# A front written out as one order, with two engines computing the modulation vectors in turn

## The chip, the core and the metric

The kernel runs on one NeuronCore of a Trainium2 chip. TensorE (PE) multiplies, VectorE (DVE), ScalarE (ACT) and GpSimd (POOL) work beside it, and SyncE (SP) and GpSimd issue DMAs. Each engine takes its own instructions in order, and engines meet only at semaphores. Times are device microseconds (us) of one launch; the metric is the median over runs. Everything is float32, and a float32 matmul of the program stands in the trace as two matmul records. A change of less than about 0.2% of the time can't be told from none here.

## The reference

One sample of 512 latent tokens and 256 context tokens, width 1024, two layers. Every layer makes six modulation vectors (shift, scale, gate, twice) from the condition vector:

```python
sh1, sc1, g1, sh2, sc2, g2 = jnp.split((silu_c @ ada_w[l] + ada_b[l])[:, None, :], 6, axis=-1)
h = modulate(x, sh1, sc1)                      # rms_norm(x) * (1 + scale) + shift
if l % 2 == 0:
    y, y_c = even_mixer(h, modulate(ctx, csh1, csc1), ...)   # differential attention, spatial gating
else:
    y = conformer_conv(h, *conv_p)
x = x + g1 * y
x = x + g2 * peer_ffn(modulate(x, sh2, sc2), ...)
```

`even_mixer` projects to q, k, v, u and vg. For each of 4 heads it takes two softmaxes over 768 keys and multiplies `p0 - lam * p1` by v; the result is normalized per head, set beside the gated `u * mixed(vg)`, and projected by `w_out`. `peer_ffn` scores each token against 2 x 128 keys for 8 heads, takes the best 16 experts of 16384 per head, and for each token reads 128 rows of two tables (`w_down` and `w_up`, 8 KB for the pair), takes a dot product, a gelu, and a weighted sum.

## The kernel before

A class `Plan` makes a list of stages, each cut into phases, and `run_phases` walks this list on every engine, so that the list sets the order of work on all of them. Phases that stand beside a gather are issued on ACT and DVE two gathers later than on PE (`later`, `LOOK = 2`).

**The main loop.** For each layer and each block of 128 tokens there are 128 gathers. A gather is one indirect DMA on POOL's queue (128 rows of 8 KB) into one of 8 slots of `ring`, a dot product on DVE, three small activations on ACT (gelu, weight, a diagonal matrix `diag`), and 4 matmuls in 64x64 tiles on PE, which sum into `ffn_out`. `beside` puts the phases of the next block (norm, q projection, gating, attention, output projection, norm, selection of experts) between the gathers, spaced by the phases' costs. `attend` has 10 phases: in the phase of head h, DVE finds the peaks of head h+1's scores, waits for ScalarE's exponentials and combines the two softmaxes, while PE waits for head h's result, turns it and later multiplies it by v.

**The front.** Until the first gather of block 0, `ring` holds other things: `ht_all` (the modulated, turned inputs of all 6 token tiles), the context, and buffers for the modulation weights. It does, in this order: `ada` (shift and scale of layer 0, four 2 MB weight chunks through PE in 64x64 tiles), `front_norms`, `lam`, keys and values of 6 tiles in turn, q, gating, attention and projection of block 0, norm, selection. Beside it runs `side_ada`, the ten other modulation vectors: 20 chunks of 2 MB, each loaded by POOL's queue into one of two buffers and summed over its 8 slices of 128 input channels by DVE alone; PE only sums over partitions afterwards (four 128x2 products, or a 128x512 one for gate rows):

```python
for k in range(KD):
    weight, scale = buffers[c.buf][:, k, :], cond_silu[:, 0, k:k + 1]
    ...
        ins = dve.scalar_tensor_tensor(out=acc_j, in0=weight, scalar=scale, in1=acc_j,
                                       op0=ALU.mult, op1=ALU.add)
    step(ins)
```

The phases of `side_ada` are spread over the others by `spread`. All other weights (2 MB chunks) go through SP's queue into `weights`, which has 2 buffers; a chunk is loaded once the one before it in its buffer has been used. POOL's first gather waits for all of `side_ada` and for the first half of the selection. PSUM has three two-bank tiles used in rotation, and a fourth for the side work.

In the prediction "u0" to "u19" are the phases of the side work in the changed kernel, k0 to k12, v, q, a, g, p, n, s those of the keys, values, query, attention, gating, projection, norm and selection.

## Time and profile before

| | before |
|---|---|
| median of 3 runs | 3370.67 us (3367.43 to 3374.5) |
| profiled execution | 3375.42 us, of which the span 3373.6 us |
| first product of the keys | 72.7 us |
| first gather issued | 361.8 us |
| PE, DVE, ACT, POOL busy | 70%, 67%, 37%, 34% |
| moved by DMA | 1288.62 MB, mean 382 GB/s |
| mean granted TensorE clock | 0.787 of 2.4 GHz |

The busy shares are means over two parts that have little in common: the front, where few gathers can run, and the main loop after it. The stages must be read apart.

### The profile page before, as it was taken

Reading aid. Unit: us, or ns where it says so; the run is one execution under the profiler, and the core shown is the slowest. Engines: PE = TensorE matmul, PEld = TensorE weight load, DVE = VectorE, ACT = ScalarE, POOL = GpSimd, SP = SyncE. Lnnn points to the kernel's source line nnn. Section 1 sums busy time; section 2 is a strip of 40 time slices with the busy share of each in tenths; the row PEclk is TensorE's granted clock in tenths of the full one; section 3 lists DMA queues with packets and bytes.
Section 4 is the critical chain, followed back from the end, with each engine's and each line's share of the span. In section 5 each row is a group of like instructions: output and inputs, shape, how many; then the busy total and the mean of one; then the engine's idle time right before and its main releaser. Section 6 shows DMA issues by size and latency. Waiting matters only on the chain.

```text
span 3373.6 us, 37863 instructions
## 1 busy us (share of the span) xinstructions
PE 2348.5 (70%) x12920; PEld 992.8 (29%) x12920; DVE 2271.6 (67%) x5467; ACT 1250.3 (37%) x3679; POOL 1132.1 (34%) x1052
## 2 busy tenths in 40 slices
PE   5966577857776778596586695675577567766676
PEld 2435223512342234262133161251124112421111
DVE  2765855685648665847947749669956896595444
ACT  2111245334533463443343442333343333343333
POOL 0000233343333333333433433333433343344332
PEclk7977688878887789797787696786788677876666
DMA  6565899999999999999999999899999999999998
GB/s 256 217 257 195 341 391 370 421 404 418 377 422 419 398 372 414 385 379 402 421 382 421 413 388 394 336 402 384 421 389 418 421 420 377 422 420 418 421 421 354
DMA packets 167025, 1288.62 MB, mean 382 GB/s; under 512 B 19248, under 2 KB 20144, under 8 KB 23728
## 3 DMA queue, kind: packets, MB, share of 16 engines
q0 software_dynamic: 150912, 1124.14, 81.9%
q1 hardware_dynamic: 15920, 162.07, 11.5%
q8 instruction: 101, 1.65, 0.2%
q14 instruction: 92, 0.75, 0.1%
HBM read 1284.04 MB, written 2.10 MB: 381 GB/s over the span
## 4 chain that ended last, share of the span: by engine, by line
DVE 30%; DMA 27%; PE 27%; issue 8%; ACT 7%; POOL 1%; DVEq 0%; ACTq 0%; SPq 0%; POOLq 0%
DMA ring<-in_experts,expert 24%; DVE ring L1340 11%; PE psum L1645 10%; DVE arena L1226 7%; PE psum L1395 6%; PE psum L1409 3%; PE psum L1591 3%; PE psum L1376 1%; DMA x<-in_x 1%; ACT arena L804 1%; DVE arena L1252 1%; POOL ring L692 1%; ACT arena L855 1%; PE psum L1561 1%; ACT shares_of L942 1%
## 5 line engine op out<-in xcount | busy, mean ns | idle before, releaser
L1645 PE MATMUL psum<-ring,diag 64*64 64x512 f32 x8192 | 1395.1, 797 | 790.5 <-ACT diag L943 781.9
L692 POOL DMA_INDIRECT ring<-in_experts,expert x1024 | 1119.0, 1093 | 1927.2 <-PE psum L1645 1757.3
L1340 DVE CUSTOM_DVE_ANT_0 ring<-ring,h 128x1024 f32<-128x1024 f32 x1024 | 1220.3, 1222 | 640.5 <-DMA ring<-in_experts,expert 623.3
L1645 PEld LDWEIGHTS psum<-ring,diag 64*64 64x64 f32 x8192 | 301.0, 163 | 1733.2 <-ACT diag L943 1484.4
L941 ACT ACTIVATE acts<-dots 128x1 f32<-128x1 f32 x1024 | 206.2, 201 | 1577.7 <-DVE dots L1340 1525.6
L943 ACT ACTIVATE diag<-ident_half,shares_of 128x64 f32<-128x64 f32 x1024 | 356.0, 348 | 33.3
L942 ACT ACTIVATE shares_of<-acts,gate 128x1 f32<-128x1 f32 x1024 | 301.7, 295 | 33.2
L1409 PE MATMUL psum<-arena,weights 128*128 128x128 f32 x2048 | 270.4, 296 | 30.1 <-DMA weights<-in_chunks 30.1
L1409 PEld LDWEIGHTS psum<-arena,weights 128*128 128x128 f32 x2048 | 259.1, 209 | 83.3 <-issue 47.8
L1226 DVE SCALAR_TENSOR_TENSOR arena<-kept,taps,arena 128x128 f32<-128x128 f32 x960 | 263.2, 343 | 2.3
L1395 PE MATMUL psum<-weights,arena 128*128 128x512 f32 x400 | 188.7, 616 | 3.6 <-ACTq L807 2.5
L718 ACT ACTIVATE arena<-psum 128x128 f32<-128x128 f32 (+2 forms) x86 | 64.6, 751 | 214.5 <-PE psum L1409 88.9
L1376 PE MATMUL psum<-ident,arena 128*128 128x128 f32 x464 | 90.2, 355 | 59.7 <-DVE arena L1082 36.0
L1591 PE MATMUL psum<-arena,weights 128*128 128x256 f32 x512 | 119.4, 386 | 0.6 <-ACTq L807 0.6
L1395 PE MATMUL psum<-weights,ring 128*128 128x512 f32 x240 | 110.6, 615 | 2.4 <-DMA weights<-in_chunks 1.8
L677 POOL DMA_DIRECT2D ring<-in_chunks x23 | 12.4, 539 | 288.1 <-DVEq L1070 266.4
L1395 PEld LDWEIGHTS psum<-weights,arena 128*128 128x128 f32 x400 | 74.0, 195 | 114.3 <-issue 106.4
L1591 PEld LDWEIGHTS psum<-arena,weights 128*128 128x128 f32 x512 | 94.9, 190 | 39.1 <-issue 24.4
L1376 PEld LDWEIGHTS psum<-ident,arena 128*128 128x128 f32 x464 | 72.2, 185 | 114.9 <-DVE arena L1082 52.9
L941 ACT ACT_TABLE_LOAD x63 | 80.8, 1283 | 5.8 <-ACT arena L718 3.1
L1340 DVE DVE_READ_ACCUMULATOR2_ANT dots<- 128x1 f32 x1024 | 82.7, 81 | 0.0
L1395 PEld LDWEIGHTS psum<-weights,ring 128*128 128x128 f32 x240 | 46.4, 197 | 57.4 <-issue 55.4
(172 smaller groups left out, 1486.3 us busy)
## 6 DMA issues: line engine op xcount, KB each, us to landing
weights<-in_chunks SPq DMA_DIRECT2D x70, 2048.0 KB
ring<-in_chunks POOLq DMA_DIRECT2D x23, 2048.0 KB, 8.7
ring<-in_experts,expert POOLq DMA_INDIRECT x1024
weights<-in_chunks SPq DMA_DIRECT2D x16, 512.0 KB
kept<-in_chunks POOLq DMA_DIRECT2D x1, 2048.0 KB, 24.1
x<-in_x SPq DMA_DIRECT2D x1, 2048.0 KB, 40.2
out_x<-x SPq DMA_DIRECT2D x4, 512.0 KB
ring<-in_ctx SPq DMA_DIRECT2D x1, 1024.0 KB, 24.3
```

The source lines that it names most:

```text
L692: pool.indirect_dma_start(out=ring[:, k, :], out_offset=None, in_=table, in_offset=bass.IndirectOffsetOnAxis(ap=expert[:, s.b % 2, n:n + 1 ...
L718: step(act.activation(dst, src, ACT.Copy))
L941: step(act.activation(acts[:, k:k + 1], dots[:, k:k + 1], ACT.Gelu))
L942: step(act.activation(shares_of[:, k:k + 1], acts[:, k:k + 1], ACT.Copy, scale=gate[:, s.b % 2, n:n + 1]))
L943: act.activation(diag[:, k, :], ident_half[:], ACT.Copy, scale=shares_of[:, k:k + 1]).then_inc(diag_ready, 1)
L1226: dve.scalar_tensor_tensor(out=acc[:, k, :], in0=z_t[:, k, w + s.b * P:w + (s.b + 1) * P], scalar=taps[:, k, w:w + 1], in1=acc[:, k, :], o ...
L1340: dve.tensor_tensor_reduce(out=ring[:, k, 0:D], in0=ring[:, k, 0:D], in1=h2[:, s.b % 2, :], scale=1.0, scalar=0.0, op0=ALU.mult, op1=ALU.a ...
L1376: ins = pe.transpose(psum[:, t.bank, k * P:(k + 1) * P], src[:, k * P:(k + 1) * P], ident[:])
L1395: ins = pe.matmul(dst, left[:, k, :], buffers[c.buf][:, k, :], start=k == 0 and begin, stop=k == KD - 1, skip_group_check=not begin)
L1409: ins = pe.matmul(dst, buffers[c.buf][:, k, g * P:(g + 1) * P], right[:, k, :], start=k == 0, stop=k == KD - 1)
L1591: ins = pe.matmul(psum[:, t.bank, 2 * g * P:2 * (g + 1) * P], buffers[c.buf][:, k, g * P:(g + 1) * P], h_pair[:, k, :], start=k == 0, stop ...
L1645: pe.matmul(ffn_out[rows_out, r * COLS:(r + 1) * COLS], diag[rows_in, k, :], ring[rows_in, k, D + n * COLS:D + (n + 1) * COLS], start=Fals ...
```

## The change

- The front is one string, `FRONT`, which sets every phase by hand. The keys come first; the values stand between the attention steps; gating stands inside the attention.
- `attend` has 13 phases (`ATTEND`): scores, turn and output of a head are phases of their own. DVE takes the peaks in the score phase and combines in the turn phase, on fewer instructions (one 128x768 pass and one small one less; the first softmax's scale moves into ScalarE's copy of the output). This holds in the main loop too.
- The side work is 24 units of 2 MB (`unit`). PE does the even ones of the 20 (and the four of `ada`) by matmuls with 32 columns, one for each of 4 column groups of the array and each half of the chunk; DVE does the odd ones as before. A unit is loaded in two halves of 1 MB. The first 8 halves have buffers of their own, and all later ones share two (`SIDE = 2`), so that a half of one unit is loaded once the same half of the unit before it has been used by the other engine. The freed place becomes a third buffer of `weights` until the gathers begin (`place`).
- POOL's queue loads only unit 0 before `x` and the context have landed.
- The modulation in `norm` is halved: ACT does 4 of the 8 slices, DVE 4.
- The even `project` is done in two halves of the inner dimension: the gated half as soon as it is there, the attention half when it comes (`half_linear`). vg is projected before u.

```diff
-    DUOS = 3
-    BUFS = 2
-    EARLY = 2
-    FIRST = 2
+    DUOS = 3
+    BUFS = 2
+    SIDE = 2
+    FIRST = 8
...
+    def unit(self, layer, sec, j, by, both=False):
+        u = Unit(len(self.units), layer, sec, j, by, both, not both and sec in (G1, G2) and layer == 0)
+        self.units.append(u)
+        u.halves = []
+        for h in range(2):
+            n = 2 * u.n + h
+            buf = n if n < self.FIRST else n % self.SIDE
+            before = self.units[(n - self.SIDE if n >= self.FIRST + self.SIDE else n % self.FIRST) // 2] if n >= self.FIRST else None
...
+ATTEND = [("score", 0), ("score", 1), ("turn", 0), ("out", 0), ("score", 2), ("turn", 1), ("out", 1), ("score", 3), ("turn", 2),
+          ("out", 2), ("turn", 3), ("out", 3), ("end", 0)]
...
+FRONT = """
+k0 k1 f3 l0 u0 k2 f4 k3 u1 k4 k5 u2 k6 k7 u3 k8 k9 u4 k10 k11 u5
+q0 q1 k12 u6 v0 v1 q2 u7 a0 v2 v3 u8 a1 v4 v5 u9 a2 v6 v7 u10 v8 v9 u11 v10 v11
+a3 a4 a5 g0 g1 u12 a6 g2 g3 a7 a8 u13 g4 a9 a10 p0 a11 u14 a12 p1 p2 u15 u16 p3 p4 p5
+n0 u17 n1 u18 n2 u19 s0 s1 u20 s2 s3 u21 s4 s5 s6 u22 s7 s8 s9 s10 s11
+"""
...
-            before = plan.early_chunks[2]
-            sp.wait_ge(landed[before.buf], before.landed)
+            sp.wait_ge(side_landed[5], 16)
...
+            for u in plan.units:
+                if u.n == 1:
+
+                    pool.wait_ge(x_landed, 32)
+                for h, (buf, there, before) in enumerate(u.halves):
+                    if before:
+                        pool.wait_ge(side_used[before[0]], before[1])
+                    pool.dma_start(side_bufs[buf].rearrange("p k n -> p (k n)"),
+                                   A["chunks"][ADA_CH[u.layer] + 2 * u.sec + u.j, :, h * 2048:(h + 1) * 2048]).then_inc(side_landed[buf], 16)
...
+                for i in range(n + 3):
+                    if i < n and s.parts[i].by == "pe":
+                        u = s.parts[i]
+                        if u.made:
+
+                            pe.wait_ge(side_line["pe"], u.made)
+                        for h, (buf, there, before) in enumerate(u.halves):
+                            pe.wait_ge(side_landed[buf], there)
+                            for k in range(KD // 2):
+                                pe.matmul(side_a[32 * k:32 * (k + 1), :], cond_wide[:, 4 * h + k, :], side_bufs[buf][:, k, :], start=h == 0,
+                                          stop=h == 1).then_inc(side_used["pe"], 1)
+                    if 2 <= i < n + 2:
+                        out(s.parts[i - 2])
+                    yield
...
+                for what, h in ATTEND[:-1]:
+                    if what == "score":
+                        peaks(h)
+                    elif what == "turn":
+                        combine(h)
                     yield
```

**VectorE while the keys are made.** What stands there before: one latent tile of the keys (the rows that end in `rope_cos` and `rope_sin`; `sumsq` is their sum of squares), between pieces of the side work (`cond_silu`), two side chunks to each tile.

```order
L1065 SCALAR_TENSOR_TENSOR ring<-ring,cond_silu 128x512 x7
L1090 TENSOR_REDUCE sumsq<-arena 128x8
L1092 RECIPROCAL rstd<-std 128x8
L1093 TENSOR_TENSOR arena<-arena,rstd 128x512
L1105 TENSOR_TENSOR arena<-arena,gains 128x512
L1106 TENSOR_TENSOR arena<-arena,rope_cos 128x512
L1111 TENSOR_TENSOR arena<-arena,rope_sin 128x16x16 x2
L1114 TENSOR_TENSOR arena<-arena 128x512
L1063 TENSOR_SCALAR h2<-ring,cond_silu 128x512
L1065 SCALAR_TENSOR_TENSOR h2<-ring,cond_silu,h2 128x512 x7
```

What stands there in the changed kernel, from the second of two key tiles on:

```order
L1155 TENSOR_REDUCE sumsq<-arena 128x8
L1157 RECIPROCAL rstd<-std 128x8
L1158 TENSOR_TENSOR arena<-arena,rstd 128x512
L1170 TENSOR_TENSOR arena<-arena,gains 128x512
L1171 TENSOR_TENSOR arena<-arena,rope_cos 128x512
L1176 TENSOR_TENSOR arena<-arena,rope_sin 128x16x16 x2
L1179 TENSOR_TENSOR arena<-arena 128x512
L1122 TENSOR_SCALAR ring<-ring,cond_silu 128x512
L1124 SCALAR_TENSOR_TENSOR ring<-ring,cond_silu 128x512 x7
```

Two key tiles now stand to one side unit, and the unit stands behind the second of them.

**TensorE at the same place.** Before, with keys and values in turn (`weights,ring` 128x512, 8 to a tile), the side work there is the sum over partitions (`ones`, four 128x2):

```order
L1395 MATMUL psum<-weights,ring 128x512 x8
L1462 MATMUL psum<-ones,h2 128x2 x4
L1395 MATMUL psum<-weights,ring 128x512 x8
L1376 MATMUL psum<-ident,arena 128x128 x4
L1462 MATMUL psum<-ones,h2 128x2 x4
```

The changed kernel, keys of tiles 3 and 4, and the side units about them (`ring,arena` 32x512 are a PE unit's products over its 1024 input channels):

```order
L1496 MATMUL psum<-h2,ones 128x512
L1467 MATMUL psum<-weights,ring 128x512 x8
L1439 MATMUL psum<-ident,arena 128x128 x4
L1515 MATMUL psum<-ring,arena 32x512 x8
L1500 MATMUL psum<-chosen,ring 128x2 x4
L1467 MATMUL psum<-weights,ring 128x512 x8
```

A PE unit stands in PE's own order between two key tiles, so that what is behind it on PE waits for its halves to land.

**TensorE in the main loop, block 1's attention.** Before (`ring,diag` are a gather's 4 products, `kept,arena` 128x512 and 128x256 the scores, `ident,arena` x6 the turn, `kept,arena` 128x128 the product with v), a head's scores and the turn of the head before it stand in one piece:

```order
L1546 MATMUL psum<-kept,arena 128x512
L1546 MATMUL psum<-kept,arena 128x256
L1546 MATMUL psum<-kept,arena 128x512
L1546 MATMUL psum<-kept,arena 128x256
L1376 MATMUL psum<-ident,arena 128x128 x6
L1645 MATMUL psum<-ring,diag 64x512 x8
L1561 MATMUL psum<-kept,arena 128x128 x6
L1645 MATMUL psum<-ring,diag 64x512 x12
```

In the changed kernel there are two gathers between them:

```order
L1595 MATMUL psum<-kept,arena 128x512
L1595 MATMUL psum<-kept,arena 128x256
L1595 MATMUL psum<-kept,arena 128x512
L1595 MATMUL psum<-kept,arena 128x256
L1702 MATMUL psum<-ring,diag 64x512 x8
L1439 MATMUL psum<-ident,arena 128x128 x6
L1702 MATMUL psum<-ring,diag 64x512 x8
L1611 MATMUL psum<-kept,arena 128x128 x6
```

## Rows read from the trace of the kernel before

**Rows 1.** The page, the queue that carries the gathers: packets, MB, share.

```profile
q0 software_dynamic: 150912, 1124.14, 81.9%
```

**Rows 2.** Stretches: us, busy (x instructions) of each engine, PEclk, DMA share, GB/s.

```profile
72.70:211.70 139.00, 127.43 (x373) 63.89 (x373) 108.92 (x174) 24.68 (x45) 6.86 (x13) 0.94 0.66 257
211.70:268.70 57.00, 30.57 (x114) 20.92 (x113) 27.51 (x55) 15.45 (x28) 0.53 (x1) 0.67 0.18 74
...
361.80:3373.60 3011.80, 2089.55 (x11816) 830.15 (x11816) 2055.64 (x5035) 1180.06 (x3550) 1119.03 (x1024) 0.78 0.98 400
```

**Rows 3.** The same for 20 us: attention of blocks 1 to 3, and an undisturbed stretch.

```profile
500.00:520.00 20.00, 14.31 (x104) 5.96 (x104) 13.89 (x26) 13.45 (x33) 9.41 (x9) 1.00 0.94 367
520.00:540.00 20.00, 11.11 (x68) 5.39 (x66) 10.06 (x20) 11.85 (x28) 6.09 (x7) 0.83 0.89 350
540.00:560.00 20.00, 14.20 (x93) 7.84 (x94) 14.04 (x25) 12.08 (x30) 6.84 (x7) 0.80 0.85 310
...
900.00:920.00 20.00, 17.74 (x112) 8.68 (x112) 12.31 (x22) 12.42 (x34) 9.06 (x10) 0.82 0.87 317
...
1240.00:1260.00 20.00, 16.25 (x120) 8.20 (x116) 13.88 (x26) 14.45 (x37) 10.09 (x8) 0.91 0.79 304
...
3140.00:3160.00 20.00, 12.73 (x68) 2.01 (x64) 9.98 (x17) 6.76 (x24) 7.50 (x8) 0.76 1.01 422
```

**Rows 4.** The chain that ended last, in order of time: start us, us, what.

```profile
3.08 40.23 DMA x<-in_x
...
137.85 7.99 DMA ring<-in_chunks
```

**Rows 5.** Timeline: start us, us, engine, line, op, out<-in, xcount, [idle before <-releaser].

```profile
25.57 3.66 PE L1431 MATMUL psum<-ring,h 64*64 64x512 f32 x32
...
58.87 3.65 PE L1376 MATMUL psum<-ident,arena 128*128 128x128 f32 x16
...
64.78 2.91 ACT L757 ACTIVATE ring<-psum,ctx_mod 128x128 f32<-128x128 f32 x8 [13.49 <-DVEq L1034]
```

**Rows 6.** Timeline within keys and values, and at their end (PE and DVE).

```profile
163.86 3.60 PE L1395 MATMUL psum<-weights,ring 128*128 128x512 f32 x8
...
165.13 0.69 DVE L1090 TENSOR_REDUCE sumsq<-arena 128x8 f32<-128x512 f32 x1 [1.70 <-ACT arena L825]
...
167.29 0.95 PE L1462 MATMUL psum<-ones,ring 128*128 128x2 f32 x8
...
169.88 0.48 DVE L1063 TENSOR_SCALAR h<-ring,cond_silu 128x512 f32<-128x512 f32 x1
...
170.39 5.47 DVE L1065 SCALAR_TENSOR_TENSOR h<-ring,cond_silu,h 128x512 f32<-128x512 f32 x7
...
197.84 1.84 PE L1462 MATMUL psum<-ones,ring 128*128 128x2 f32 x8 [8.05 <-DVEq L1047]
...
201.99 9.77 PE L1395 MATMUL psum<-weights,ring 128*128 128x512 f32 x16
```

**Rows 7.** Timeline from the projection's result to the first gather.

```profile
289.58 1.23 DVE L1189 TENSOR_TENSOR arena<-psum,g_row 128x1024 f32<-128x1024 f32 x1 [3.50 <-PE psum L1395]
...
293.92 0.75 DVE L1082 TENSOR_SCALAR arena<-x,rstd 128x1024 f32<-128x1024 f32 x1
...
311.97 3.82 PE L1409 MATMUL psum<-arena,weights 128*128 128x128 f32 x32
...
332.48 1.64 DVE L1248 MAX8 top_v<-arena 128x8 f32<-128x128 f32 x8 [3.52 <-ACTq L720]
...
361.80 0.98 POOL L692 DMA_INDIRECT ring<-in_experts,expert  x1 [60.35 <-issue]
```

**Rows 8.** Timeline of PE, a head of block 2's attention in the main loop.

```profile
879.73 1.99 PE L1645 MATMUL psum<-ring,diag 64*64 64x512 f32 x8 [6.38 <-ACT diag L943]
...
886.64 1.57 PE L1546 MATMUL psum<-kept,arena 64*128 64x512 f32 x8
...
897.26 1.98 PE L1645 MATMUL psum<-ring,diag 64*64 64x512 f32 x8 [6.37 <-ACT diag L943]
```

More of the change, by code:

```diff
@@ L90, in __init__, with claim, read @@
         self.first, self.last = first, last
+        self.claims, self.needs, self.dones = {}, {}, {}
         self.cost = cost
+    def claim(self, phase, *tiles):
+        self.claims.setdefault(phase, []).extend(tiles)
+    def read(self, chunk, first, last, tile, part):
+        self.needs.setdefault(first, []).append(chunk)
+        self.dones.setdefault(last, []).append(chunk)
+        chunk.last_use = (tile, part)
 class Plan:
@@ L190, in front_norms @@
         s.tile = [self.tile() for _ in range(NT)]
+        for i in range(NT // 2):
+            s.claim(1 + i, *s.tile[2 * i:2 * i + 2])
         return s
@@ L202, in norm, with heads @@
         s.ht = self.take("ht_ready")
+        s.half = self.take("half_ready")
         s.tile = self.tile()
+        s.claim(1, s.tile)
         if dest:
             s.back = self.tile()
+            s.claim(2, s.back)
             s.h2 = self.take("h2_ready")
         return s
-    def heads(self, name, tiles, source, beside=None, first=False):
+    def heads(self, name, tiles, source, first=False):
         s = Stage("heads", name=name, tiles=tiles, first=first, cost=(3.6, 4) * len(tiles) + (2,))
@@ L214, in heads @@
         s.chunk = self.chunk(source)
-        s.proj, s.turn = [None] * len(tiles), [None] * len(tiles)
-        for n in range(len(tiles) + 1):
-            if n < len(tiles):
-                s.proj[n] = self.tile()
-            if n:
-                s.turn[n - 1] = self.tile()
-            if n < len(tiles) and beside:
-                beside.proj[n] = self.tile()
-        self.used(s.chunk, s.proj[-1], 0)
+        s.proj, s.turn = [self.tile() for _ in tiles], [self.tile() for _ in tiles]
+        for n in range(len(tiles)):
+            s.claim(2 * n, s.proj[n])
+            s.claim(2 * n + (3 if n + 1 < len(tiles) else 2), s.turn[n])
+        s.read(s.chunk, 0, 2 * len(tiles) - 1, s.proj[-1], 0)
+        s.before, self.turned = self.turned, s.turn[-1]
         s.copied = self.take("qk_copied", len(tiles))
@@ L295, in conv_in @@
         for j in range(4):
-            self.used(s.chunks[j], s.out[j], 0)
+            s.claim(4 * j, s.out[j])
+            s.read(s.chunks[j], 4 * j, 4 * j + 3, s.out[j], 0)
         s.sig = self.take("sig_ready", 2)
@@ L415, in phases_of @@
     return phases
-def spread(p, phases, side):
-    room = [ROOM[s.kind][n] if s.kind in ROOM else 1 for s, n in phases]
-    done, so_far = 0, 0.0
-    for item, r in zip(phases, room):
-        p.order.append(item)
-        so_far += r
-        while done < len(side) and done < round(len(side) * so_far / sum(room), 6):
-            p.order.append(side[done])
-            done += 1
+FRONT = """
[4 more added lines that the diff above has]
+"""
 def make_plan():
@@ L471, in make_plan @@
     p.beside(1, 3, [])
+    p.place()
     return p
@@ L1118, in gating @@
             def gating(s):
-                for _ in range(3):
-                    yield
+                u, vn = gated(s)
+                yield
                 t = s.vt
@@ L1384, in rows, with half_linear @@
                 return ins
+            def half_linear(t, j, left, c, part):
+                pe.wait_ge(landed[c.buf], c.landed)
+                for k in range(4 * part, 4 * part + 4):
+                    ins = pe.matmul(psum[:, t.bank, j * COLS:(j + 1) * COLS], left[:, k, :], buffers[c.buf][:, k, :], start=k == 4,
+                                    stop=k == 3, skip_group_check=True)
+                if part == 0:
+                    ins.then_inc(full[t.bank], 1)
             def linear(t, part, left, c, begin=True):
```

632 lines of the change are left out of this document (318 added, 314 removed).

## The prediction

> **What bounds the kernel now.** I began with the stretches [rows 2]. From the first gather at 361.8 us [rows 7] to the end, the DMA engines are busy 98% of 3011.8 us at 400 GB/s, and no compute engine passes 70%: the main loop is bound by the gathers' bytes. An undisturbed stretch moves 422 GB/s [rows 3]. The gathers' queue carries 1124 MB [rows 1], of which 24 side chunks are 50 MB, so a gather is 1.05 MB, or 2.5 us at 422 GB/s. Before 361.8 us hardly a gather can run, so each us by which the front is shorter should come off the end, and each GB/s lost in the main loop can be had back. These are the only two places where time can be found.
>
> The front, read in order of time: `x` lands 40.2 us after its issue at 3.1, because four side chunks share the engines with it, [rows 4], and the keys begin at 72.7. From there to 211.7 PE is busy 127 of 139 us at clock 0.94; it is the bound. In the attention, 211.7 to 268.7, PE is busy 31 of 57 us at clock 0.67 and DMA stands at 18%: one head waits for the last [rows 2]. The projection's result is read at 289.6, the normalized tile is there at 294.7, the selection starts at 332.5 and the first gather goes at 361.8 [rows 7]. In the main loop the bandwidth falls in the attention of blocks 1 to 3: 367, 350, 310, then 317, then 304 GB/s [rows 3].
>
> **The change part by part.** The sum is made against the profiled execution, 3375.4 us (span 3373.6 and 1.8 around it), which lies 4.7 above the median of the runs shown.
>
> *Start.* Unit 0 (2.1 MB), context and `x` (3.1 MB) are alone now: 5.4 MB with the small ones at 425 GB/s is 13 us, landed at about 17. Units 1 to 3 and the parameters (7.7 MB) follow, landed at about 40. ScalarE's squares stand behind the copy of unit 1's row in its order and finish at about 33, which is hidden behind unit 3. Then, after unit 3: one half of products (1.2), three sums over partitions (0.95 each at the full clock, 1.84 behind a stop [rows 6], so 1.4), two turned tiles (3.65) and ScalarE's modulation (2.9) [rows 5]: 12 us. Keys start at about 52 and not 72.7: **20 us gained**; 17 to 24 by which clock PE has.
>
> *A unit on PE.* The trace has no product with 32 columns. Nearest are the 64x64 tiles: 32 records in 3.66 us, 0.11 each [rows 5], where 128-wide ones take 8 in 3.43 to 3.60, 0.43 each [rows 6]: four tiles run at once. A unit is 16 records. If four column groups run at once it is 2.2 us with two starts, if two 3.8, if none 7.0. I take 2.2, since the 64x64 tiles already overlap two column groups over the same rows; 7.0 stays for the range.
>
> *Reload of a half.* Before, a chunk of 2.1 MB took 8.0 us from issue to landing with the queues quiet [rows 4]. At 425 GB/s 4.9 of it is bytes, so 3.1 is not; half a chunk is 2.5 + 3.1 = 5.6 us. The Trainium skill (DMA: Bandwidth & Descriptors, Anatomy of one DMA) gives 2.0 us and bytes over 436 GB/s. By it a half would be 4.4 and the whole 6.8; the trace has 8.0, so the trace decides. By the page's figure the five reloads on the path below would take 6 us less.
>
> *Keys.* Here the written order makes a ring that was not there. A PE unit can't start before the DVE unit in front of it has used its halves and they have been reloaded, and the DVE unit stands behind two key tiles on DVE. From one PE unit's end to the next: its sum over partitions 0.95 to 1.8, a key linear 6.9 (two of 3.43), ScalarE's copy and square 1.7, DVE's key work 4.75 (165.13 to 169.88), DVE's unit 6.0 (0.5 + 5.5, all in [rows 6]), reload 5.6, last half 1.2: 27 to 28 us. PE has 14.6 us of key work and 3 of side work in that time, so it stands still 7 to 9 us in each. After such a stop it runs slow for a while: behind the idle 8.05 us a linear pair of 16 records took 9.77 and not 6.9, the sum 1.84 and not 0.95 [rows 6]. I add 2.5 to each: 30. The first ring is longer by two turned tiles and the start, 37. Keys start 52, u2 ends at 89, u4 at 119, u6 at 149. The query is within.
>
> *From u6 to the projection's end.* PE's own work: values 41.2 (12 x 3.43), vg and u 13.7, projection 13.7, attention 16 (four a head, of which the scores' pair is 1.6 [rows 8]), five PE units 11, sums over partitions 12, turns and gating 3: 110 us. Waits: combine behind a unit or behind the next head's peaks, at a2, a5, a8: 2, 4, 4; u13 and gating stand ahead of the last combine on DVE: 6; u16 behind u15, which themselves stand behind the last norm of the heads: 5; one copy 1: 22. Clock after five stops: 8. 149 + 140 = 289. Before it was 289.6. **The 20 us of the start are given back in the ring**, and what overlapping values with attention saves (26 idle us in the 57) pays for the five PE units, their sums, and u16.
>
> *Tail.* u17 (DVE) stands ahead of DVE's half of the modulation, and u18 (PE) ahead of the second turn. From 294.7: h1 used at 300.9, landed 306.5, u18 done 308.6 with its sum, turn 310.6, four parts of the query for the selection 3.8 to 4.4 each [rows 7], 16.7 with a side sum between, the keys' products, copies and the last side sums 6.4: the selection starts at 333.7, not 332.5, and the selection itself (29.3 us) is unchanged. First gather 363: **front +1 us**. The third weight buffer costs and gives nothing here: before, the wait for weights fell into the second half of the selection, which is hidden behind DVE's first half.
>
> *Main loop.* Before, DVE waited inside a head's phase for the exponentials and combined there, and the next gather's dot and activations stood behind that; PE then waited 6.4 us for `diag`. A head took 17.5 us (879.73 to 897.26) for 5 gathers [rows 8], which need 12.5 us of DMA: 5 too many. With combine in a phase two gathers later, the waiting, the combine and ScalarE's copy of the turned weights are off this chain. In bytes, the five attention stretches with the rates above cost 2.6, 3.4, 5.3, 5.0 and 5.6 us of their 20 against 422 [rows 3]: 22 us, with a few more beside them. The exponentials and their table load still hold ScalarE, so I take three quarters: **-16 us**; the bounds are 0 and -22. Halved modulation takes half of 2.9 us [rows 5] off ScalarE and puts about as much on DVE, beside gathers that wait for DMA: nothing; without cover it is 14 norms x 1.5 = 21 us at most. The projection's chunks are held longer, but the next is needed 9 gathers later, over 20 us: nothing.
>
> Sum: +1 - 16 = -15: 3360 for such a profile, **3356** against the median.
>
> **Rivals.**
>
> *A, the ring is looser than summed* (reload nearer 4.4, clock not lost after the stops). Then the front keeps 15 of its 20 us: 3340. For it: each addend of clock is drawn from one stop [rows 6]. Against it: the reload and the order are as they stand.
>
> *B, the main loop gives nothing*, because ScalarE's exponentials and table loads alone make the head's time. The front is level, so the time stays: 3371. This is the case in which the change moves work and not time.
>
> *C, slower: column groups do not run side by side.* A PE unit then takes 7.0, not 2.2. Of the 4.8 more, half shows in units whose first half is covered by a wait (u2, u4, u6, u16, u18 and unit 3), all of it in u0 and the five others: 14 + 29, less some waits now covered: +40, and with the main loop's -16 the time is 3395. It turns from gain to loss at 2.2 + 15/8.4 = 4 us a unit. The Trainium skill (TensorEngine Tiling, Tiling Modes) has 128x32 as four independent tiles, and speaks against this rival; it also says that a change of tiling mode drains the array, which no stretch here shows alone.
>
> *D, the clock.* PE stops nine times for over 4 us and stays at the lower level longer, as in the attention before (0.67): 12 us more, 3368.
>
> **How the numbers follow.** Forecast 0.35, A 0.25, B 0.18, C 0.10, D 0.12. The likeliest gives 3356. The range takes in A with some 10 us for its bounds and D and B; of C it leaves out most: 3328 to 3384. More than 0.2% is 6.7 us. Faster: forecast most (0.32), A (0.25), a little of D: 0.62. Same: B most, half of D, some of the forecast: 0.22. Slower: C, the rest: 0.16.
>
> **What would show it.** `x` landed by 18 and keys at 49 to 56. In the keys, PE waits of 5 to 9 us ahead of u2, u4 and u6, released by a side DMA; none there, and A holds. Sixteen 32-column records in 2 to 2.5 us, else C. First gather within 350 to 375. In blocks 1 to 3 the attention stretches at over 390 GB/s, and no 6.4 us waits for `diag`; if they stand, B. The prediction is wrong if the first gather moves by over 15 us, or if GB/s falls anywhere else in the main loop, as at the norms.

## The result and the profile after

| | before | after |
|---|---|---|
| median | 3369.44 us (20 runs, 3361.41 to 3376.42) | 3380.07 us (20 runs, 3372.63 to 3391.72) |
| profiled execution | 3375.42 us | 3391.72 us, span 3389.9 |
| first product of the keys | 72.70 us | 58.65 us |
| first gather | 361.80 us | 396.32 us |
| first gather to the end | 3011.8 us | 2993.6 us |

The ratio is 1.0035, with a 95% interval of 1.0026 to 1.0043: the change costs time, 10.6 us by the medians. I had forecast 15 us of gain. Both sides of the sum are visible in the trace: the main loop gives 18 us (16 forecast), the front loses 34.5 (1 forecast). One run each of two kernels below (all side units on VectorE; four halves and sums sooner) ran at a granted clock of 0.66 and 4% longer, and the ratios leave them out.

The profiled execution of after is the longest of its 20 runs, 11.7 us above their median, and that of before lies 6.0 above its own, so profiles differ by 16.3 and medians by 10.6. The kernels of the experiments show that this profile is a bad case on both sides. Three of them share its start and its order up to the projection; they begin the projection's first tile on PE at 282.7, 283.4 and 283.9 us, after at 288.3. And ten of them share its main loop; from the first gather to the last they gain 19 to 30 us on the one profile of before, after 18. By the medians of the runs below the main loop gives 18 us (10.0 and 8.0), so the front loses about 29. A difference of 5 us between single profiles means little.

The stretches of after, as in [rows 2] (us, busy and instructions of each engine, PEclk, DMA share, GB/s): the keys, from there to the projection's end, and the main loop.

```profile
58.60:183.50 124.90, 96.59 (x296) 47.22 (x296) 55.36 (x103) 26.71 (x54) 8.44 (x16) 0.80 0.45 165
183.50:319.70 136.20, 114.44 (x416) 59.29 (x413) 44.93 (x82) 27.32 (x45) 9.49 (x18) 0.86 0.54 194
396.30:3389.90 2993.60, 2094.34 (x11816) 828.97 (x11816) 2069.11 (x5079) 1162.78 (x3497) 1125.08 (x1024) 0.79 0.98 403
```

In the keys PE now stands idle for 28 of 125 us and runs at 0.80; before, in keys and values together, it was idle for 12 of 139 us at 0.94. Who it waits for, as the view of waits has it for PE from 58 to 396 us (total us, times, longest):

```profile
PE psum L1515 <- DMA ring<-in_chunks: 19.6, 7, 5.6
PE psum L1500 <- DVEq L1108: 18.3, 4, 6.2
...
PE psum L1494 <- ACTq L801: 5.2, 2, 3.6
PE psum L1500 <- ACTq L801: 0.8, 1, 0.8
```

The first row is the wait that I had counted, for a half's reload. The other three, 24.3 us together, wait for the sums of the side work, and no term of my sum is such a wait. Before PE may sum a unit over the partitions it waits for `side_done`, until DVE (columns, L1108) or ScalarE (rows, L801) has taken up the unit before; and these do it one step later in the order, behind their key work. The timeline of PE from the first modulation to u6:

```profile
26.64 1.94 PE L1515 MATMUL psum<-ring,arena 128*32 128x512 f32 x8 [15.16 <-DMA ring<-in_chunks]
...
40.08 3.64 PE L1515 MATMUL psum<-kept,arena 128*32 128x512 f32 x16 [3.24 <-ACT arena L810]
...
56.92 1.94 PE L1439 MATMUL psum<-ident,arena 128*128 128x128 f32 x8 [1.74 <-ACTq L831]
58.65 9.18 PE L1467 MATMUL psum<-weights,ring 128*128 128x512 f32 x16
73.39 3.51 PE L1439 MATMUL psum<-ident,arena 128*128 128x128 f32 x16 [5.56 <-ACTq L831]
76.82 1.92 PE L1515 MATMUL psum<-ring,arena 128*32 128x512 f32 x16
78.68 7.13 PE L1467 MATMUL psum<-weights,ring 128*128 128x512 f32 x16
...
99.13 1.93 PE L1515 MATMUL psum<-ring,arena 128*32 128x512 f32 x8 [5.58 <-DMA ring<-in_chunks]
102.19 1.93 PE L1515 MATMUL psum<-ring,arena 128*32 128x512 f32 x8 [1.12 <-DMA ring<-in_chunks]
...
107.49 7.03 PE L1467 MATMUL psum<-weights,ring 128*128 128x512 f32 x16
...
118.55 2.05 PE L1494 MATMUL psum<-ident,ada_bias 128*128 128x128 f32 x8 [3.59 <-ACTq L801]
...
132.45 1.07 PE L1515 MATMUL psum<-ring,arena 128*32 128x512 f32 x8 [0.74 <-DMA ring<-in_chunks]
...
135.70 9.97 PE L1467 MATMUL psum<-weights,ring 128*128 128x512 f32 x16
...
152.32 1.84 PE L1500 MATMUL psum<-ones,ring 128*128 128x2 f32 x8 [6.21 <-DVEq L1108]
154.02 9.35 PE L1467 MATMUL psum<-weights,ring 128*128 128x512 f32 x16
...
163.74 1.92 PE L1515 MATMUL psum<-ring,arena 128*32 128x512 f32 x16
170.02 1.84 PE L1500 MATMUL psum<-chosen,h 128*128 128x2 f32 x8 [4.36 <-DVEq L1108]
```

To be seen: a unit's products take 1.92 us for 16 records; key tiles (x16) take 7.0 to 7.1 us at the fastest and 9 to 10 in the later turns (135.70, 154.02). Not every stop brings a slow tile: the one at 107.49 took 7.03 us behind stops of 5.58 and 1.12. And u4 (132.45) waits hardly at all for its half, since PE has been held up by the sums and the tile before it. The stops take turns.

The end of the front, DVE at the projection's result, then PE, the first gather, and what answers [rows 7]:

```profile
319.74 1.22 DVE L1252 TENSOR_TENSOR arena<-psum,g_row 128x1024 f32<-128x1024 f32 x1 [20.81 <-PE psum L1453]
...
324.07 0.75 DVE L1135 TENSOR_SCALAR arena<-x,rstd 128x1024 f32<-128x1024 f32 x1
...
325.10 1.83 PE L1500 MATMUL psum<-ones,ring 128*128 128x2 f32 x8 [5.40 <-DVEq L1108]
...
333.75 1.94 PE L1515 MATMUL psum<-ring,arena 128*32 128x512 f32 x8 [5.00 <-DMA ring<-in_chunks]
...
343.71 10.24 PE L1481 MATMUL psum<-arena,weights 128*128 128x128 f32 x64
...
366.50 1.65 DVE L1311 MAX8 top_v<-arena 128x8 f32<-128x128 f32 x8 [11.56 <-ACTq L783]
...
396.32 0.98 POOL L755 DMA_INDIRECT ring<-in_experts,expert  x1 [56.64 <-DVEq L1393]
```

In the main loop the attention of block 1 (two of its stretches; the two around them have 394 and 386 GB/s), of block 2 and of block 3, as in [rows 3]:

```profile
520.00:540.00 20.00, 14.51 (x82) 5.75 (x82) 11.60 (x21) 12.20 (x33) 6.26 (x6) 0.74 1.00 419
540.00:560.00 20.00, 14.03 (x98) 5.90 (x90) 13.14 (x24) 12.80 (x31) 8.86 (x8) 0.91 0.93 358
...
880.00:900.00 20.00, 15.87 (x97) 6.99 (x90) 12.79 (x23) 11.94 (x32) 8.87 (x8) 0.78 1.02 421
900.00:920.00 20.00, 15.87 (x115) 7.38 (x114) 14.06 (x26) 13.89 (x37) 8.96 (x9) 0.91 0.98 388
...
1240.00:1260.00 20.00, 16.15 (x110) 7.25 (x110) 9.61 (x20) 11.81 (x31) 6.75 (x8) 0.90 0.84 300
```

Block 2's two low stretches, 367 and 317 GB/s before, are at 421 and 388. Block 3's lowest is still 300.

### The profile page after: what moved, and what is told of

Its sections match the earlier page's. It is cut to its first block, busy times and chain, and to the rows that moved or that the text cites. A ratio compares the mean times of both kernels' runs of the same rounds, so it can differ in the third digit from the quotient of the medians.

```text
span 3389.9 us, 38103 instructions
## 1 busy us (share of the span) xinstructions
PE 2385.5 (70%) x13016; PEld 996.5 (29%) x13016; DVE 2222.8 (66%) x5436; ACT 1242.8 (37%) x3641; POOL 1150.8 (34%) x1076
## 4 chain that ended last, share of the span: by engine, by line
PE 32%; DVE 29%; DMA 27%; issue 6%; ACT 5%; POOL 1%; DVEq 0%; SPq 0%; ACTq 0%; POOLq 0%
DMA ring<-in_experts,expert 25%; PE psum L1702 11%; DVE ring L1403 10%; DVE arena L1289 7%; PE psum L1467 6%; PE psum L1481 5%; PE psum L1648 3%; PE psum L1439 2%; DMA ring<-in_chunks 1%; DVE arena L1315 1%; PE psum L1453 1%; POOL ring L755 1%; PE psum L1611 1%; ACT diag L1020 1%; ACT shares_of L1019 1%
## 5 line engine op out<-in xcount | busy, mean ns | idle before, releaser
L1481 PE MATMUL psum<-arena,weights 128*128 128x128 f32 x1920 | 254.2, 296 | 27.3 <-DMA weights<-in_chunks 27.2
L1481 PEld LDWEIGHTS psum<-arena,weights 128*128 128x128 f32 x1920 | 243.4, 209 | 80.4 <-issue 45.4
L1467 PE MATMUL psum<-weights,arena 128*128 128x512 f32 x272 | 131.9, 629 | 0.2 <-ACTq L876 0.2
L737 POOL DMA_DIRECT2D ring<-in_chunks x46 | 24.5, 534 | 313.7 <-DVEq L1127 155.9
L781 ACT ACTIVATE arena<-psum 128x1024 f32<-128x1024 f32 (+2 forms) x73 | 60.1, 823 | 182.2 <-PE psum L1467 100.0
L1439 PEld LDWEIGHTS psum<-ident,arena 128*128 128x128 f32 x464 | 76.3, 193 | 148.9 <-DVE arena L1225 56.0
L1648 PEld LDWEIGHTS psum<-arena,weights 128*128 128x128 f32 x512 | 94.9, 190 | 38.6 <-issue 27.0
L1216 DVE TENSOR_REDUCE peak<-psum 128x1 f32<-128x768 f32 x32 | 30.5, 952 | 97.2 <-PE psum L1595 97.1
L1467 PEld LDWEIGHTS psum<-weights,arena 128*128 128x128 f32 x272 | 51.8, 201 | 79.7 <-issue 77.8
L1467 PE MATMUL psum<-weights,ring 128*128 128x512 f32 x144 | 74.9, 680 | 0.0
## 6 DMA issues: line engine op xcount, KB each, us to landing
x<-in_x SPq DMA_DIRECT2D x1, 2048.0 KB, 14.2
```

The costliest lines, as they stand in the source:

```text
L781: step(act.activation(dst, src, ACT.Copy))
L1439: ins = pe.transpose(psum[:, t.bank, k * P:(k + 1) * P], src[:, k * P:(k + 1) * P], ident[:])
L1467: ins = pe.matmul(dst, left[:, k, :], buffers[c.buf][:, k, :], start=k == 0 and begin, stop=k == KD - 1, skip_group_check=not begin)
L1481: ins = pe.matmul(dst, buffers[c.buf][:, k, g * P:(g + 1) * P], right[:, k, :], start=k == 0, stop=k == KD - 1)
L1648: ins = pe.matmul(psum[:, t.bank, 2 * g * P:2 * (g + 1) * P], buffers[c.buf][:, k, g * P:(g + 1) * P], h_pair[:, k, :], start=k == 0, stop ...
```

## The experiments

Theory 1: the front is held by the two half buffers and by the late taking up of the sums, at the start by an order that puts ScalarE's squares behind a copy, and at the end by units put inside the norm; the main loop's gain comes from the attention. Its rival, theory 2: products of the side work on PE don't pay at all, whatever the buffers. A third: the reload is short and nothing here binds; the front is PE's own work at a low clock.

**The finer attention alone**, on the kernel before. The front, the side work and the weight buffers are those of before.

```diff
-        s = Stage("attend", b=b, cost=(8,) + (8, 2) * (HEADS - 1) + (2, 2, 4))
+        s = Stage("attend", b=b, cost=tuple({"score": 4, "turn": 2.5, "out": 2.5, "end": 4}[what] for what, h in ATTEND))
...
-                for h in range(HEADS):
-                    if h + 1 < HEADS:
-                        peaks(h + 1)
-                        combine(h + 1)
-                    yield
+                for what, h in ATTEND[:-1]:
+                    if what == "score":
+                        peaks(h)
+                    elif what == "turn":
+                        combine(h)
```

> The kernel before with the finer attention alone (13 steps, the scores of head h written as soon as head h-2 is through, the cheaper combining); the order of its front, the side matmuls and the two weight buffers are those of before. My theory: the main loop's 18 us that the trace of the changed kernel shows come from the attention alone, so this run gains them and loses nothing in the front: about 3369 - 18 = 3351 us, the first gather near 362 us as before, and the 20-us attention stretches of the main loop shorter. Rival: the finer attention gives little without the written order around it or costs in the front's own blocks what it gives later: 3369 us within 4. Second rival: the 18 us come from the third weight buffer's earlier arena loads, then the main loop stays at 3012 us.

Measured: 3359.47 us, 0.9968 of before (0.9955 to 0.9981). The first gather stays at 361.57 us, the main loop falls by 11.3 us, not by 18, and the time is 8 us above my forecast. So the attention is faster by itself and harmless in the front, but it is not all of the main loop's gain.

**Four half buffers** in place of two; the third weight buffer, whose place they take, goes.

```diff
-    SIDE = 2
+    SIDE = 4
...
-                open_to = range(self.BUFS + (last[c] < gathers[0]))
+                open_to = range(self.BUFS)
```

> The changed kernel with four half buffers for the side weights in place of two, and without the third weight buffer, whose space they take. Theory A (the ring of two halves sets the front: a half comes free only when the unit before last is through, and its reload then takes 5.6 us or more): the waits of 4.7 to 5.6 us of PE on a half's chunk go, u6 ends about 10 us earlier, the first gather comes 10 to 20 us earlier, 3360 to 3370 us. Theory B (what sets the front is the hand-over of the sums, DVE's and ScalarE's rows queued behind key work, and the late start): the chunk waits turn into waits on the sums, the first gather moves by under 4 us: 3376 to 3382 us. If the third buffer is what carries the front's projection, the run is slower than the changed kernel by 3 to 8 us.

Measured: 3347.47 us, 0.9926 (0.9913 to 0.9939), first gather 364.66. These two edits turn the loss of 10.6 into a gain of 22. That is more than I expected of them.

**No third weight buffer**, still two halves (the second edit above without the first), to take this part out.

> The changed kernel without the third weight buffer, still with two half buffers: it takes the removal of the third buffer out of the run with four halves. Theory A (the third buffer is worth nothing in the front, as forecast; the 32 us of the four halves come from the halves alone): first gather 394 to 400 us, 3378 to 3384 us. Theory B (the third buffer hurt: its loads share the engines with the halves' reloads or its chunk's last use holds the gathers): first gather below 390 us, under 3374 us.

Measured: 3377.16 us, 1.002 (1.0011 to 1.0029), first gather 388.80: the gather is in theory B's range, the time between the two, 2.9 us better by the medians. The third buffer gives nothing and may cost a few us. It does cover one wait: without it PE stands 4.4 us in the selection for a chunk of weights, where after does not, and the gather comes no later for it.

```profile
PE psum L1479 <- DMA weights<-in_chunks: 4.4, 1, 4.4
```

The two profiles drift apart from the first key tile on (7.51 us here, 9.18 after), where the third buffer plays no part yet, and the run with the norm undone (below), which keeps it, has its first gather at 389.50 too. So most of the 7.5 us of the gather is the clock of a single execution. The four halves are worth 30 us against this kernel by the medians.

**The sums taken up in the step in which PE writes them**, not one later, by DVE and by ScalarE.

```diff
-                    if i >= 3 and not s.parts[i - 3].row:
-                        u = s.parts[i - 3]
+                    if 2 <= i < n + 2 and not s.parts[i - 2].row:
+                        u = s.parts[i - 2]
```

> The changed kernel with VectorE and ScalarE taking up a unit's sums in the step in which PE writes them, not one step later, so that PE's next sums don't wait for a VectorE that is behind with key work. Nothing else is moved. Theory A (this hand-over holds PE: 19.3 us over six waits for VectorE's rows and 5 for ScalarE's): the waits go and the first gather comes 6 to 15 us earlier, 3365 to 3374 us. Theory B (the halves' ring sets the pace, the wait for the sums only takes a part of a wait for the chunk that would come anyway): the waits turn into waits on the chunks, 3376 to 3380 us.

Measured: 3382.48 us, 1.0042 (1.003 to 1.0054), first gather 395.27: theory B, nothing. The view of waits, PE from 58 to 395 us, shows why: all waits for the sums are gone, and the chunks have taken every us of them.

```profile
PE psum L1515 <- DMA ring<-in_chunks: 44.0, 11, 9.8
```

**Both together.**

> The changed kernel with four half buffers (two weight buffers) and the sums taken up a step sooner. Alone the halves moved the first gather from 396.3 to 364.7 us, the sums sooner only to 395.3. Theory A (the two waits cover each other: with two halves, PE waits for a chunk where it no longer waits for VectorE, 67 us on chunks instead of 43; with four halves the chunk is there and the wait for the sums, 21 us over eight, is bare): first gather at 348 to 356 us, 3331 to 3340 us. Theory B (the sums sooner give nothing in any setting, the 12 us by which the four edits together beat the sum of the four alone have another source, such as the clock or the start): first gather 361 to 365 us, 3344 to 3349 us.

Measured: 3331.7 us, 0.9874 (0.9857 to 0.9891), first gather 340.17: theory A by the time, and 8 us earlier than it had the gather. What was worth 0 alone is worth 16 us by medians (24 by the gather) on top of four halves.

**The start**: the norms before the second chunk, and f3 before k1.

```diff
-    p.order += [(first, 0), (first, 1), (norms, 0), (first, 2),
+    p.order += [(first, 0), (norms, 0), (first, 1), (first, 2),
...
-k0 k1 f3 l0 u0 k2
+k0 f3 k1 l0 u0 k2
```

> The changed kernel with two transpositions at the start: the norms stand ahead of the second chunk of the first modulation, and the first block's fourth chunk ahead of the second key step. Theory A (the late start, keys at 58.7 us where 52 was forecast, and the first side unit at 76.8 where 62 was forecast, is carried through to the first gather): the front loses 6 to 12 us of its 34, 3368 to 3374 us. Theory B (the front is set by rings and waits later on, which swallow an earlier start): first gather within 3 us of the changed kernel's, 3377 to 3381 us.

Measured: 3369.95 us, 1.000 (0.999 to 1.001), first gather 384.31: theory A, at its far end. In PE's timeline the wait of 5.56 us is gone, and u0 is at 65.86, not 76.82:

```profile
56.61 4.14 PE L1467 MATMUL psum<-weights,ring 128*128 128x512 f32 x8
60.59 1.91 PE L1439 MATMUL psum<-ident,arena 128*128 128x128 f32 x16
62.33 3.60 PE L1467 MATMUL psum<-weights,ring 128*128 128x512 f32 x8
65.86 1.92 PE L1515 MATMUL psum<-ring,arena 128*32 128x512 f32 x16
```

**The tail**: units out of the norm and out of the projection's middle.

```diff
-a12 p1 p2 u15 u16 p3 p4 p5
-n0 u17 n1 u18 n2 u19 s0 s1 u20 s2 s3 u21 s4 s5 s6 u22 s7
+a12 p1 u15 p2 p3 p4 p5 u16
+n0 n1 n2 u17 s0 s1 u18 s2 u19 s3 u20 u21 s4 u22 s5 s6 s7
```

> The changed kernel with the side units moved out of the last norm and out of the gap between the projection's parts: 'p1 u15 p2 p3 p4 p5 u16 n0 n1 n2 u17 s0 s1 u18 s2 u19 ...'. Theory A (the last five units stand on the chain: idle times of 4.7, 5.4, 5.0 and 1.1 us of PE there): the first gather comes 6 to 12 us earlier, 3368 to 3374 us. Theory B (the units are bound by their ring of two halves wherever they stand): the waits move into the selection, under 3 us gained, 3377 to 3381 us.

Measured: 3364.34 us, 0.9991 (0.9982 to 1.0), first gather 377.47: more than theory A had, and not where I had put it. The projection's result is there at 300.34 instead of 319.74. Of these 19.4 us 4.4 are there before the first step that was moved (the projection's first tile starts at 283.90, in after at 288.34), so the edit holds about 15, near the 15.7 of the medians: u16 no longer stands between the projection's parts, with waits of 4.74 and 1.25 us for its halves (PE at 300.98 and 304.17 in after), its own products and sums, and a tile of 6.61 us behind it that takes 3.70 here. From there to the first gather it takes 77.1 us, and 76.6 in after: moving the units out of the norm gave nothing, their waits went along. First the tile that took 6.61 us in after, then such a wait:

```profile
293.17 3.70 PE L1453 MATMUL psum<-ring,arena 128*128 128x512 f32 x8 [0.80 <-ACTq L783]
...
339.37 1.83 PE L1500 MATMUL psum<-chosen,ring 128*128 128x2 f32 x8 [6.96 <-DVEq L1108]
```

**All side units on VectorE**, and **all on TensorE**, with two halves:

```diff
-"dve" if j else "pe") for layer, sec in sections
+"dve") for layer, sec in sections
```

> The changed kernel with all side units on VectorE, so that PE makes no side products; the order of the steps is the same. Theory A (turns between the two engines are what costs: each engine's unit waits for the other's sums and half): PE's waits on the side's sums vanish, but VectorE's side work of about 10 us a unit doubles; VectorE then bounds the front: slower than the changed kernel by 10 to 40 us, 3390 to 3420 us. Theory B (VectorE had enough idle time in the front, and the alternation gives nothing): 3370 to 3380 us.

> The changed kernel with all side units on TensorE and none on VectorE, same order, still two half buffers. All on VectorE brought the first gather from 396.3 to 369.4 us. Theory A (what costs is that turns of the two engines share two halves: a unit of the one can be loaded only when the other's, queued behind its own work, is through): with one engine alone the ring is shorter in the same way, VectorE is relieved of its 10 units, and the first gather goes to 365 to 375 us: 3350 to 3358 us. Theory B (products on TensorE are what costs, since they stand in PE's own order, each waiting for a half that is reloaded in 5.4 us): PE waits for a chunk at each of the 20 units; the first gather stays at 390 us or goes later, 3375 to 3390 us.

Measured: all on VectorE 3360.23 us, 0.9967 (0.9954 to 0.998), first gather 369.36, which neither theory had; all on TensorE 3370.29 us, 1.0007 (0.9998 to 1.0015), first gather 379.67, between the two theories. Turns with two halves are worse than either engine alone. On VectorE alone PE waits for no chunk after 58 us, but 47 us for the sums. All on TensorE with four halves was not run.

**All four edits together** (four halves, sums sooner, start, tail).

> The changed kernel with four half buffers (and two weight buffers), the two transpositions at the start, the side units moved out of the norm, and the sums taken up a step sooner, all four together. Alone, four halves gave 33 us and the start 10. Theory A (they are separate waits, each on the same chain): the first gather comes at 335 to 350 us, before the 361.8 of the kernel before, 3322 to 3338 us. Theory B (they all remove the same slack, beneath which lies PE's own work of about 290 us of 362): first gather 352 to 362 us, 3335 to 3346 us.

Measured: **3309.73 us**, 0.9832 (0.9819 to 0.9845), first gather 320.00. This is the version that beats both kernels, by 59 us and 70 us, further than theory A went. The first gather comes 76.3 us earlier than in after; the four edits alone moved it by 31.7, 1.1, 12.0 and 18.9, 63.6 together.

**The same, all on VectorE.**

> The kernel with all four edits (first gather at 320.0 us) with all side units on VectorE. With two halves, all on VectorE was 27 us better in the front than the turns. Theory A (turns were bad only because the two engines shared two halves and PE's sums stood behind VectorE; with four halves they are good, since VectorE does a unit in 6 us and up and PE in 1.9): all on VectorE loses: first gather 330 to 345 us, 3320 to 3335 us. Theory B (products on PE never pay, since they stand in the order of the engine that bounds the front): first gather 312 to 320 us, 3302 to 3310 us.

Measured: 3336.71 us, 0.9904 (0.9889 to 0.9919), first gather 347.34: theory A, a little beyond it. With four halves, turns are worth 27 us over VectorE alone; theory 2 falls.

What these say together, for PE from 58 us to the first gather. "Side waits" are the waits for chunks and for sums, summed from the view of waits; busy and clock are from the stretch from 58 us to the gather, three of whose rows follow the table.

```
                     side waits (chunks + sums)   PE busy   clock   stretch
after                19.6 + 24.3 = 43.9           263.4     0.82    338
no third buffer      21.3 + 23.5 = 44.8           255.6     0.85    331
sums sooner          44.0 +  0                    253.4     0.82    337
four halves           0   + 27.0                  251.2     0.87    307
both                  7.0 +  0                    237.7     0.90    282
all four edits        0   +  2.8                  226.0     0.94    262
```

After:

```profile
58.00:396.00 338.00, 263.42 (x1077) 153.50 (x1075) 145.15 (x329) 65.40 (x115) 20.05 (x38) 0.82 0.50 184
```

No third buffer:

```profile
58.00:388.80 330.80, 255.63 (x1072) 149.56 (x1070) 145.12 (x329) 65.50 (x115) 20.05 (x39) 0.85 0.53 193
```

All four edits:

```profile
58.00:320.00 262.00, 226.03 (x1069) 134.56 (x1067) 142.85 (x321) 62.61 (x107) 18.94 (x36) 0.94 0.63 237
```

It is the same work (some 1070 records). Of the 76 us between after and the last line, 41 are waits for the side work and 37 are the same matmuls at a higher clock; the other waits about cancel out. After's 263.4 us stand alone, though: four kernels with 44 to 45 us of side waits (no third buffer, sums sooner, the start, norm and order undone) were busy for 253.4 to 255.7. Against the kernel without the third buffer it is 69 us to the last line, 42 of them side waits and 30 busy time. Step by step the two don't keep a fixed ratio: four halves take away 18 us of side waits and 4 us of busy time, the sums on top of them 20 and 14. Theory 3 was half right: the low clock costs 30 us or more beside 42 us of stops, but it comes with them.

**The main loop: the norm on ScalarE alone again, the projection behind the attention again.** Undone in the changed kernel.

```diff
-    for late, n, after, m in (("heads", 2, "gating", 1), ("gating", 4, "attend", 0), ("attend", len(ATTEND) - 1, "project", 0)):
+    for late, n, after, m in (("heads", 2, "gating", 1), ("gating", 4, "attend", 0)):
...
-                for k in range(KD // 2):
+                for k in range(KD):
```

> The changed kernel with two parts undone: the modulation of a norm is done by ScalarE alone again, and the projection's first step stands behind the attention's last, not ahead of it. The finer attention stays. From the first gather to the last the changed kernel takes 17 to 25 us less than the kernel before, the kernel before with the finer attention alone 10. Theory A (these two parts make the difference): the main loop comes to within 4 us of 3000.5 us, that of the finer attention alone. Theory B (the difference comes from elsewhere, the projection in six steps and the gating's order, or from the state of the memory at the start of the main loop): the main loop stays at 2986 to 2994 us. The front may lose up to 4 us by the undone norm.

Measured: 3388.11 us, 1.0054 (1.004 to 1.0068), first gather 389.50, main loop 2996.5 us, 4.0 from that of the finer attention alone: theory A, at its bound. Where it goes is seen by counting gathers: us from the first gather to the nth behind it in the kernel before, and the difference to it in the others (from POOL's timeline).

```
  nth   before    after    start   attention alone   norm and order undone
   64    193.2    -11.4    -11.7    -13.5             -11.2
  192    568.7    -19.4    -21.4    -12.8             -14.1
  320    967.0    -17.9    -21.3     -9.8              -5.6
  640   1959.1    -18.6    -25.5    -10.8              -9.3
 1023   2984.9    -18.1    -26.5    -11.1             -15.3
```

In after the gain is made by the 192nd gather and kept. By medians the attention alone is worth 10.0 us, and undoing the other two parts costs 8.0 (3388.11 against 3380.07). The front's own norm shows no part in it: without its halving the gather is at 389.50, in the kernel without the third buffer at 388.80. At the 640th gather the profile has 9.3 for them, at the last one only 2.8. But after is again at the edge. Counting in all eleven kernels that have the changed main loop, the difference is -18.0 to -23.1 at the 192nd gather, -17.7 to -23.3 at the 320th and -18.1 to -30.4 at the last. With the two parts undone it is -14.1, -5.6 and -15.3. So at the 320th gather the two parts hold at least 12 us, clear of the scatter, and over the whole loop a difference of 10 us between single profiles means nothing.

## Why the prediction was wrong

*The start* (20 us gained, keys at 52). `x` landed at 17.3 as said (14.2 us after its issue at 3.08), but the keys began at 58.65, so 14 us were gained, and u2 ended at 104.1, not 89 (100.1 to 103.2 in the three kernels with the same start). ScalarE's squares, which I had "hidden behind unit 3", stand from 31.60 to 37.9 behind unit 1's copy, and PE's unit 3 waited 3.24 us for the copy that stood behind them. And I had no term for a wait before the turns of tiles 4 and 5: they stand 5.56 us until ScalarE has modulated the tile before them, behind its work on the first keys. Two transpositions brought 10 of these us back, by the medians. This step failed by size, 11 to 15 us.

*The ring* (30 us a turn, a stop of 7 to 9 us). Ends of units: u2 104.1, u4 133.5, u6 165.7, thus 29.4 and 32.1. The length came out right in part by luck. I had forecast a wait of 5 to 9 us for a side DMA ahead of each of u2, u4 and u6; the trace has 5.58 and 1.12 ahead of u2, 0.74 ahead of u4 and none ahead of u6. PE's stops within the two turns are 4.3 and 7.0 us, nearly all for the sums. The rest of the length is work: the first turn has two sums of gate rows of 3.4 and 3.5 us, where I had counted 0.95 to 1.8, and the second two key tiles of 9.97 and 9.35 us. (The stop of 7 to 9 doesn't follow from my own terms either: 27 to 28 less 14.6 and 3 is 9.4 to 10.4. Nothing in the sum rests on it.) I had one wait, for the half, where there are two in parallel, each long enough to hide the other. The runs on halves and sums show it.

*A unit on PE* (2.2 us): 1.92. Rival C is refuted. The Trainium skill (TensorEngine Tiling, Tiling Modes) has four independent tiles of 128x32, and the trace agrees: 16 such records take 1.92 us, 16 of full width 7.03. *The reload* (5.6): 5.4 at the median of 46.

*From u6 to the projection's end* (work 110, waits 22, clock 8: 140 us). It took 154: 319.7 less 165.7; 151.5 in the kernel without the third buffer. The list of waits had neither the sums nor the clock that they cost. For u16 behind u15 I had 5 us; its waits of 4.74 and 1.25 are near that, but the tile behind it takes 6.61 instead of 3.70 us, and moving u15 and u16 gave 15 us back, their own work included.

*The tail* (+1): from the end of the normalized tile (324.82) to the first gather 71.5 us, where I had 68.3 and the kernel before 67.1. The waits of 5.40 and 5.00 us ahead of u17's sums and for u18's half are in it. Moved elsewhere they came up again, so they belong to the ring and not to the place.

*The main loop* (-16; 0 to -22): -18.2 in the profile of after and 18.0 by the medians of the two runs on it, right in size. The eleven profiles with this main loop scatter from -18 to -30, seven of them beyond my bound of -22, but all are taken against one profile of before that lies 6.0 above its own median. The cause was right for the larger part, 10 us by the medians; I had put nothing on the halved norm and the projection, and by the runs they hold about 8. From 860 to 960 us PE now waits 9.9 us for `diag`, five times, 5.3 at the longest; before it was 27.2, seven times, up to 6.4. The stretches over 390 GB/s came in block 2 (one at 388), not wholly in block 1 (358, 386) and not in block 3.

The step that fails is therefore "**The 20 us of the start are given back in the ring**", with the "front +1" that is added up from it. Of the 33 us by which the gather (396.3) misses my 363, some 15 are the start, 2 the two turns, 14 the way from u6 to the projection's end and 3 the tail. The sum took start and ring as an even exchange; in fact the start gave 14, and the two half buffers together with the late sums cost 48 us by the medians (3380.07 against 3331.70). Without them the first gather comes at 340.17, 23 us before my forecast of 363. The forecast held the waits between the queues to be one chain, summed once, and left out the second, the waits for the sums.

It also charged the clock at 2.5 us a ring and 8 behind it, some 15 us, where busy time falls by 30 us (against the kernel without the third buffer) to 37 us (against after) once the side waits are gone. Rival D (the clock stays low, 12 us more) named this, and with its 12 the charge would have been of about the right size. But even so D lies below the kernel before: of my rivals only C made the change a loss, and for another reason.

## What to carry to other kernels

When two engines take turns on one pair of buffers, each load waits for the slower engine's whole queue; before counting the ring, ask what a second pair costs, since it was worth 30 us here. Where an engine waits in turn on two others, list both waits at every turn: mending one alone shows nothing, and the shorter is bare once the longer is gone, so test them together before either is given up. Price a stop on TensorE above its length where the granted clock is low around it: here 30 to 37 us of busy time came back with 41 or 42 us of stops, though not evenly from one step to the next. And before reading a part's size off one profile, look where other kernels with the same part stand: after's own profile had the projection some 5 us too late and the main loop's gain at the low end of eleven.

## What the runs showed of the hardware

The products with 32 columns in four column groups take 1.92 to 1.94 us for a unit of 16 records of 128x512, or for only 8 of them behind a stop; 16 records of full width take 7.0 to 7.1. So the four groups run side by side nearly in full.

The granted clock goes with stops of a few us each. From 58 us to the first gather it rose from 0.82 to 0.94 as the waits for the side work fell from 43.9 to 2.8 us, and the same 1070 or so records took 263 or 226 us. The five kernels with 44 to 45 us of such waits, after among them, had 0.82 to 0.85 and 253 to 263 us, so one execution can stand 8 us from its like, for which I have no cause.

A load of 1 MB by POOL's queue landed 5.4 us after its issue (the median with two halves); in the three kernels with four halves in turns it was 6.7 to 7.5, with four halves all on VectorE 5.4 again. One of 2 MB took 8.3 us by SyncE's queue and 8.7 by POOL's in the kernel before.
